# Forgetting attention in another order: long and short units in turn, negated scores with a running minimum, forget sums spread by one product of 40 rows

## The reference, cut to what matters

```python
q, k, v, z, f_logit = split(h @ w_in)                  # q, k, v: 8 heads x 128; f_logit: one per head
log_f = log_sigmoid(f_logit + b_f)
c = cumsum(log_f, axis=tokens)
s = einsum('bqhd,bkhd->bhqk', q_i, k) * 1/sqrt(128)    # for each block of 128 queries
logits = where(k_pos <= q_pos, s + c_q - c_k, -inf)
p = softmax(logits)
o = einsum('bhqk,bkhd->bqhd', p, v)
y = (o * silu(z)) @ w_out
```

## Time and profile before

| | |
|---|---|
| time, median of 3 runs | 2329.61 us (2328.22 to 2335.32) |
| the profiled execution's own time | 2328.99 us |
| its span in the trace | 2327.3 us, 29119 instructions |
| busy share of TensorE, VectorE, ScalarE, GpSimd | 95%, 48%, 37%, 18% |
| attention block: first score product to end of the last group's copy | 1586.37 to 1647.76 us |

### The profile page before, as it was taken

How to read it: one execution, slowest core, us unless ns; L and a number is a source line. 1 busy time by engine, 2 the same in 40 slices (tenths; PEclk the granted TensorE clock), 3 DMA queues, 4 the chain that set the end, 5 groups by cost and what they waited for, 6 DMA issues and landing times. The chain is left out here.

```text
span 2327.3 us, 29119 instructions
## 1 busy us (share of the span) xinstructions
PE 2208.1 (95%) x10778; PEld 1772.1 (76%) x10778; DVE 1124.9 (48%) x1810; ACT 855.8 (37%) x1407; POOL 417.6 (18%) x461
## 2 busy tenths in 40 slices
PE   7999999999889999998899989999999997999988
PEld 6888887766667888887788878886778887876657
DVE  5444324423436444324475544337656784655443
ACT  4322223443334322223432232135446743433453
POOL 2111002113333111001120010001100341014441
PEclk8999999999989999999899999999999997999999
DMA  4333333511022333331333246740243220242202
GB/s 136 115 92 98 93 100 84 95 46 55 19 73 73 108 91 99 91 99 52 103 98 90 82 76 108 98 80 1 73 119 82 55 55 20 76 97 60 52 19 67
DMA packets 359321, 182.10 MB, mean 78 GB/s; under 512 B 41926, under 2 KB 356015, under 8 KB 358831
## 3 DMA queue, kind: packets, MB, share of 16 engines
q1 hardware_dynamic: 359214, 180.69, 30.6%
HBM read 176.14 MB, written 4.52 MB: 78 GB/s over the span
## 5 line engine op out<-in xcount | busy, mean ns | idle before, releaser
L313 PE MATMUL ps<-xh,wh 128*128 128x512 f32 x1920 | 768.3, 400 | 12.9 <-DVE wl L280 10.9
L315 PE MATMUL ps<-xh,wl 128*128 128x512 f32 x1920 | 750.7, 391 | 0.0
L314 PE MATMUL ps<-xl,wh 128*128 128x512 f32 x1920 | 750.0, 391 | 0.0
L280 DVE TENSOR_TENSOR wl<-raw,wh 128x1024 fp32r<-128x1024 f32 x334 | 422.7, 1267 | 437.4 <-ACT wh L270 432.6
L270 ACT ACTIVATE wh<-raw 128x1024 fp32r<-128x1024 f32 x334 | 342.1, 1027 | 363.9 <-PE ps L315 332.6
L313 PEld LDWEIGHTS ps<-xh,wh 128*128 128x128 f32 x1920 | 361.9, 188 | 104.2 <-issue 18.2
L315 PEld LDWEIGHTS ps<-xh,wl 128*128 128x128 f32 x1920 | 361.6, 188 | 77.6
L314 PEld LDWEIGHTS ps<-xl,wh 128*128 128x128 f32 x1920 | 362.4, 189 | 73.6 <-issue 2.4
L457 PE MATMUL ps<-xh,wh 128*128 128x512 f32 x304 | 132.2, 435 | 26.2 <-ACT xh L392 15.5
L450 POOL TENSOR_TENSOR acc<-acc,sq 128x512 f32<-128x512 f32 x72 | 102.4, 1423 | 275.9 <-ACT sq L835 178.0
L314 PE MATMUL ps<-a_lo,wh 128*128 128x512 f32 x352 | 137.0, 389 | 0.0
(11 more groups left out here) (379 smaller groups left out, 2527.4 us busy)
## 6 DMA issues: line engine op xcount, KB each, us to landing
raw<-in_w_ffn_gate SPq DMA_DIRECT2D x44, 512.0 KB, 3.8
raw<-in_w_ffn_up SPq DMA_DIRECT2D x44, 512.0 KB, 3.8
raw<-in_w_ffn_down SPq DMA_DIRECT2D x32, 512.0 KB, 3.6
raw<-in_conv_w_in SPq DMA_DIRECT2D x32, 512.0 KB, 4.0
raw<-in_fox_w_in SPq DMA_DIRECT2D x32, 512.0 KB, 9.6
raw<-in_gdn_w_in SPq DMA_DIRECT2D x32, 512.0 KB, 4.1
raw<-in_w_in SPq DMA_DIRECT2D x24, 512.0 KB, 3.8
raw<-in_swa_w_in SPq DMA_DIRECT2D x32, 256.0 KB, 3.8
```

Source lines behind the costliest of these rows:

```text
L280: nc.vector.tensor_tensor(wl[s][:, 0:kb, :], raw[r][:, 0:kb, :], wh[s][:, 0:kb, :].bitcast(F32), ALU.subtract).then_inc(lo_done, 1)
L313: pe.matmul(o, wh[s][:, kb, :], x_hi, start=start, stop=False)
L314: pe.matmul(o, wh[s][:, kb, :], x_lo, start=False, stop=False)
L315: return pe.matmul(o, wl[s][:, kb, :], x_hi, start=False, stop=stop)
```

## The change

What it does, part by part:

- The order of the units: within each half of four heads, first k = 4 and k = 1 in turn (k = 4 of a head, k = 1 of the same head, then the next head), then k = 3 and k = 2 in turn. The group of a unit is given with the unit, and the groups end at other steps. Heads 4 to 7 are spread at steps 12, 14, 16 and 18 in place of 14, 15, 16 and 17.
- The sign: q is scaled by -128 ** -0.5, `nsel` holds +1 in place of -1, the mask fills +1e30. So Z is the negated score, the reduction takes the minimum, which is the negated maximum, and the exponential has scale -1. The instruction that negated the maximum (L1109) goes, and ScalarE waits for the reduction itself (`z_done`). `pair_steps` keeps its own instruction, and counts the semaphore from its own base (`n["maxima"]`, three lines not shown).
- The spread: the running sum is split by VectorE into a rounded high part and a rounded low part (three new instructions: copy, subtraction, copy, each of 8 x 512), on partitions 0 to 7 and 32 to 39 of `fhl`. `nsel` gets 40 rows with the selecting ones in both places, by two clears of zeros and two selects on GpSimd, and the product is one F32R instruction. The row of ones for the running sum is a broadcast of `ones`.

```diff
@@ -1052,16 +1052,12 @@
             U = len(units)
             Z, PT = room[:, 0:4, :], room[:, 4:6, :]
             SC, TR, PV = banks
-            cols = sb(f"{name}_cols", [P, 4, U], ctx=ctx)
-            MX, NM, RS, RI = range(4)
+            cols = sb(f"{name}_cols", [P, 3, U], ctx=ctx)
+            NM, RS, RI = range(3)
             B, BG = n["units"], n["groups"]
             n["units"] += U
             n["groups"] += len(groups)
-            group_of, start = {}, 0
-            for g, (last, _, _) in enumerate(groups):
-                for u in range(start, last + 1):
-                    group_of[u] = g
-                start = last + 1
+            group_of = {u: d["group"] for u, d in enumerate(units)}
             last_of = {last: g for g, (last, _, _) in enumerate(groups)}
             def pe_step(pe, s):
@@ -1104,10 +1100,7 @@
                     if u >= 4:
                         dve.wait_ge(t_done, B + u - 3)
                     nc.vector.tensor_tensor_reduce(Z[:, u % 4, 0:d["klen"]], ps[SC[u % len(SC)]][:, 0:d["klen"]], d["mask"],
-                                                   1.0, NEG, ALU.add, ALU.max, cols[:, MX, u:u + 1]).then_inc(z_done, 1)
-                    dve.wait_ge(z_done, B + u + 1)
-                    nc.vector.tensor_scalar(cols[:, NM, u:u + 1], cols[:, MX, u:u + 1], -1.0, None,
-                                            ALU.mult).then_inc(nm_done, 1)
+                                                   1.0, -NEG, ALU.add, ALU.min, cols[:, NM, u:u + 1]).then_inc(z_done, 1)
                 if 1 <= s < U + 1:
                     u, d = s - 1, units[s - 1]
                     dve.wait_ge(p_done, B + u + 1)
@@ -1120,9 +1113,9 @@
             def act_step(act, s):
                 if s < U:
                     u, d = s, units[s]
-                    act.wait_ge(nm_done, B + u + 1)
+                    act.wait_ge(z_done, B + u + 1)
                     z = Z[:, u % 4, 0:d["klen"]]
-                    nc.scalar.activation(z, z, ACT.Exp, bias=cols[:, NM, u:u + 1],
+                    nc.scalar.activation(z, z, ACT.Exp, bias=cols[:, NM, u:u + 1], scale=-1.0,
                                          accum_out=cols[:, RS, u:u + 1]).then_inc(p_done, 1)
                 if 2 <= s < U + 2:
                     u, d = s - 2, units[s - 2]
...
@@ -1811,9 +1805,11 @@
         with ExitStack() as c:
             qkv = sb("fox_qkvz", [P, 4 * DB, SEQ], ctx=c)
             vt = sb("fox_v", [P, TB, D], ctx=c)
-            fl = sb("fox_f", [H8, 4, SEQ], ctx=c)
+            fl = sb("fox_f", [H8, 3, SEQ], ctx=c)
             bf = sb("fox_bf", [H8, 1], ctx=c)
-            nsel = sb("fox_nsel", [H8, H8, P], ctx=c)
+            LO = 32
+            nsel = sb("fox_nsel", [LO + H8, H8, P], F32R, ctx=c)
+            fhl = sb("fox_f_parts", [LO + H8, SEQ], F32R, ctx=c)
             decay = sb("fox_decay", [P, 4, SEQ], ctx=c)
             f_in, fsel, fd, decay_mm, decay_in, bias_in = (sem(f"fox_{x}") for x in ("bf", "sel", "f", "rows", "decay", "bias"))
             ev0 = n["ev"]
@@ -1824,11 +1820,15 @@
             def pool_tail(pool):
-                nc.gpsimd.memset(nsel[:, :, :], 0.0).then_inc(fsel, 1)
-                nc.gpsimd.memset(fl[:, 3, :], 1.0).then_inc(fsel, 1)
-                pool.wait_ge(fsel, 1)
-                nc.gpsimd.affine_select(out=nsel[:, :, :], in_=nsel[:, :, :], compare_op=ALU.not_equal, fill=-1.0, base=0,
-                                        pattern=[[-1, H8], [0, P]], channel_multiplier=1).then_inc(fsel, 1)
+                nc.gpsimd.memset(nsel[:, :, :].bitcast(F32), 0.0).then_inc(fsel, 1)
+                nc.gpsimd.memset(fhl[:, :].bitcast(F32), 0.0).then_inc(fsel, 1)
+                pool.wait_ge(fsel, 2)
+                for part in range(2):
+                    if part:
+                        pool.wait_ge(fsel, 3)
+                    nc.gpsimd.affine_select(out=nsel[:, :, :], in_=nsel[:, :, :].bitcast(F32),
+                                            compare_op=ALU.not_equal, fill=1.0, base=-LO * part,
+                                            pattern=[[-1, H8], [0, P]], channel_multiplier=1).then_inc(fsel, 1)
             def f_evac(dve, i, j, ev0_):
                 if isinstance(i, int) and 4 * i + j == 28:
@@ -1842,7 +1842,7 @@
                 if 28 <= k < 32:
                     turn[0](pe, 2 * (k - 28), 2 * (k - 28) + 2)
                 if k >= 31:
-                    pe.wait_ge(fd, 6)
+                    pe.wait_ge(fd, 9)
                     for hd in (2 * (k - 31), 2 * (k - 31) + 1):
                         spread_decay(pe, hd)
@@ -1852,25 +1852,31 @@
                 if k in (28, 31):
                     q = qkv[:, 4 * (k > 28):4 * (k > 28) + 4, :]
                     dve.wait_ge(evac, ev0 + 8)
-                    nc.vector.tensor_scalar(q, q, P ** -0.5, None, ALU.mult)
+                    nc.vector.tensor_scalar(q, q, -(P ** -0.5), None, ALU.mult)
                 if k == 29:
                     dve.wait_ge(f_in, 16)
                     dve.wait_ge(evac, ev0 + 29)
                     nc.vector.tensor_scalar(fl[:, 0, :], fl[:, 0, :], bf[:, 0:1], None, ALU.add).then_inc(fd, 1)
                 if k == 30:
-                    dve.wait_ge(fsel, 3)
+                    dve.wait_ge(fsel, 4)
                     dve.wait_ge(fd, 4)
                     nc.vector.scalar_tensor_tensor(out=fl[:, 2, :], in0=fl[:, 0, :], scalar=0.0, in1=fl[:, 1, :],
                                                    op0=ALU.min, op1=ALU.subtract).then_inc(fd, 1)
                     dve.wait_ge(fd, 5)
-                    nc.vector.tensor_tensor_scan(fl[:, 0, :], fl[:, 3, :], fl[:, 2, :], 0.0, ALU.mult, ALU.add).then_inc(fd, 1)
+                    nc.vector.tensor_tensor_scan(fl[:, 0, :], ones[0:H8, 0:1].broadcast_to([H8, SEQ]), fl[:, 2, :], 0.0, ALU.mult, ALU.add).then_inc(fd, 1)
+                    dve.wait_ge(fd, 6)
+                    nc.vector.tensor_copy(fhl[0:H8, :], fl[:, 0, :]).then_inc(fd, 1)
+                    dve.wait_ge(fd, 7)
+                    nc.vector.tensor_tensor(fl[:, 1, :], fl[:, 0, :], fhl[0:H8, :].bitcast(F32), ALU.subtract).then_inc(fd, 1)
+                    dve.wait_ge(fd, 8)
+                    nc.vector.tensor_copy(fhl[LO:LO + H8, :], fl[:, 1, :]).then_inc(fd, 1)
             def spread_decay(pe, hd):
                 if hd >= 2:
                     pe.wait_ge(decay_in, hd - 1 if hd < 5 else hd)
-                pe.matmul(ps[7 if hd > 3 else 6 + hd % 2][:, :], nsel[:, hd, :], fl[:, 0, :], start=True, stop=True).then_inc(decay_mm, 1)
+                pe.matmul(ps[7 if hd > 3 else 6 + hd % 2][:, :], nsel[:, hd, :], fhl[:, :], start=True, stop=True).then_inc(decay_mm, 1)
             def copy_decay(act, hd):
                 act.wait_ge(decay_mm, hd + 1)
@@ -1901,18 +1907,19 @@
                     evac_dve=f_evac, loop_end=7)
             with ExitStack() as c2:
-                order = [(half, qb, hd) for half in range(2) for qb in range(TB) for hd in range(4 * half, 4 * half + 4)]
+                order = [(half, qb, 4 * half + x) for half in range(2) for two in ((3, 0), (2, 1)) for x in range(4) for qb in two]
+                done_order = [(half, qb) for half in range(2) for qb in (3, 0, 2, 1)]
                 bias_slot = [qkv[:, 22 + x, :] for x in range(2)]
                 units = []
                 for u, (half, qb, hd) in enumerate(order):
                     klen = (qb + 1) * P
                     units.append(dict(
                         q=qkv[:, hd, qb * P:qb * P + P], k=qkv[:, 8 + hd, 0:klen], klen=klen,
-                        mask=bias_slot[u % 2][:, 0:klen], mask_ready=(bias_in, u + 1), po=0, m=P,
+                        mask=bias_slot[u % 2][:, 0:klen], mask_ready=(bias_in, u + 1), po=0, m=P, group=done_order.index((half, qb)),
                         oc=(hd % 4) * P, v=[vt[:, x, hd * P:hd * P + P] for x in range(qb + 1)]))
-                second = {4 * TB + x - 2: 4 + x for x in range(4)}
+                second = {4 * TB + 2 * x - 4: 4 + x for x in range(4)}
                 def spread_second(pe, s):
                     if s in second:
@@ -1920,11 +1927,11 @@
                 def copy_second(act, s):
                     if s in second:
-                        act.wait_ge(bias_in, s + 2)
+                        act.wait_ge(bias_in, s - 2)
                         copy_decay(act, second[s])
-                groups = [(4 * g + 3, F[:, 4 * (g // TB):4 * (g // TB) + 4, (g % TB) * P:(g % TB) * P + P],
-                           lambda b: b[:, :].rearrange("p (a q) -> p a q", a=4)) for g in range(2 * TB)]
+                groups = [(order.index((half, qb, 4 * half + 3)), F[:, 4 * half:4 * half + 4, qb * P:qb * P + P],
+                           lambda b: b[:, :].rearrange("p (a q) -> p a q", a=4)) for half, qb in done_order]
                 u_fox = n["units"]
                 pe_p, dve_p, act_p = softmax_attention("fox", units, groups, qkv[:, 16:22, :], c2, spread_second, copy_second)
```

(9 more changed lines are left out.)

## The result

The changed kernel takes 2334.19 us in the median (2331.81 to 2342.11, 20 runs) against 2328.87 us for the kernel before beside it (2327.47 to 2335.32, 20 runs): the ratio is 1.0026, with a 95% interval of 1.002 to 1.0033. That is slower by 5.3 us, and within the 0.3% that were called no change; 2332.2 had been predicted.

A forecast was written before the change was run, and what follows sets the result against it. A two-unit cycle through ScalarE was taken to bound the block; start to 1594.7, 49.0 of cycles, 0.95 of spreads and 5.75 of end gave 1650.4 against 1647.76, +2.6 us: median 2332.2, range 2325 to 2338.

The forecast's parts named there:

- The cycle: In the block, reduction of s sets reduction of s + 2: 4.20 us per 4-1 pair, 3.38 per 3-2 pair.
- rival 3: Hand-over from reduction to ScalarE keeps its price of 0.31 us: +2.1 us, 2334 us; chance 0.15.
- The spreads: Four one-instruction F32R spreads ahead of long scores in the block: 0.24 us each, 0.95 in all.
- Ahead of the block: Split on VectorE, then two spreads in 0.48 us: tile 32 starts 0.35 us earlier, bounds 0 and 0.6.
- The start: Block's start: first reduction 1.6 us behind first scores, unit 4 reduced 7.1 us later, partly at half clock.
- The end: From unit 30's reduction to the block's end: 5.75 us, ending at 1650.4.
- middle: From unit 4 to unit 30 in the block: 13 cycles of 49.0 us plus 0.95 for spreads.
- The price of the order: Units in turn cost 1.2 and 0.4 us more a pair than sorted ones, over eight pairs each.
- 1 (throughput binds): In the block, engines' throughput binds, not the cycle: pairs of 2.8 us, 9 us less, 2321 us; chance 0.06.
- 2 (the clock falls in the middle): TensorE's clock falls inside the block: +13 us in all 4-1 stretches, 2345 us; chance 0.07.
- 4 (the minimum is slower): The block's minimum reduction takes a slower form, twice its 0.62 us on 13 cycles: +7 us, 2339; chance 0.02.
- 5: VectorE's scale reaches the shared memory port ahead of GpSimd's select, some 0.1 us earlier; no change in sum, no chance given.

The follow-up runs named there:

- e1: The kernel before with the new order of units alone, keeping maximum, negation and float32 spreads: 2336.94 us, ratio 1.0042 to the kernel before.
- e3: The changed kernel with ScalarE's copy of unit s - 2 put ahead of the exponential of unit s: 2323.42 us, ratio 0.9984 to the kernel before.
- e2: The changed kernel with the old sorted order of units and old spread steps, keeping minimum and F32R spread: 2321.64 us, ratio 0.9975 to the kernel before.
- e5: The changed kernel with ScalarE's copy ahead of the exponential and block spreads ahead of short scores: 2323.69 us, ratio 0.9987 to the kernel before.
- e6: The changed kernel with the old sorted order and steps, and ScalarE's copy ahead of the exponential: 2321.63 us, ratio 0.9976 to the kernel before.
- e12: The changed kernel measured once more, unaltered: 2334.16 us, ratio 1.0027 to the kernel before on the same chip.
- e7: The kernel before with negated scores and the minimum alone, no negation instruction, old order and spreads: 2322.40 us, ratio 0.9978 to the kernel before.
- e8: The kernel before with the F32R spreads alone, keeping sorted order, maximum and negation: 2325.31 us, ratio 0.999 to the kernel before.
- e10: The changed kernel with ten unread F32R products in TensorE's idle time ahead of the block: 2334.06 us, ratio 1.0025 to the kernel before.
- e11: e6 with unread TensorE products, ten ahead of the block and others behind it: 2319.67 us, ratio 0.9962 to the kernel before.

## Why the prediction was right, and where it was off

**The cycle: right.** Long units set the pace with nothing idle between: 4.14 and 3.36 us a pair, 4.20 and 3.38 predicted. Its parts: the hand-over from the reduction is 0.12 (0.15 taken, so rival 3 with 0.31 is out), that from the copy to the values 0.05 (0.15 taken), copy, exponential and scores as priced. The values took 1.00 (0.92 taken), which ate most of what the hand-overs gave: the sum is better than its terms. e1 and e3 show it from both sides: with the negation in it a 4-1 pair takes 4.33 us, and with the copy taken out of it 3.28.

**The spreads: the mis-sized term.** "0.24 each", with up to 0.5 kept for gaps; on the cycle one takes 3.98 - 3.36 = 0.62 us, against a pair of the same sizes without one. 0.43 lie between the spread and the scores behind it, 0.1 ahead of it (values to spread 0.87, values to scores 0.77), 0.1 behind (scores to reduction 0.95 for 0.85). 24 like products in a row show 0.24 each, and don't show the price of standing alone between others. Four spreads: +1.5 us. A float32 one costs 1.25 on the same cycle (e1), so the gain is a half, not three quarters.

**Ahead of the block: right, with luck.** From running sum to first score it takes 12.38 us for 12.75, -0.37 (-0.35 predicted). Two misses cancel: the spreads start 2.88 behind the start of the running sum (3.03 taken), and both take 0.66 (0.48 taken).

**The start: off by 0.4.** The first reduction comes 1.13 behind the first score (1.6 taken), unit 4 7.93 behind unit 0 (7.1 taken). The clock fell later than before, 5 us behind the first score in place of 0.6, and the half clock covered the scores of unit 4 as well as the values of unit 0:

```profile
1589.12 2.08 PE L1087 MATMUL ps<-fox_qkvz,fox_v 128*128 128x128 f32 x8 [0.60 <-ACT fox_qkvz L1125]
1590.99 1.77 PE L1069 MATMUL ps<-fox_qkvz 128*128 128x512 f32 x2
```

They take 1.16 and 1.02 at full clock; the prediction had 1.1 for the scores. The end was right, 5.84 for 5.75.

**The sum.** Start -0.47, unit 4 +0.83, middle 50.94 for 49.96 (+0.98: the spreads' 1.5 less half a microsecond of hand-overs), end +0.09: the block is 1.4 us longer than predicted, so +4.1 for +2.6 with the scatter of the running sum taken out. That the whole came out at 2333.7 for 2331.6 is luck in part: of the profiled execution's +4.7 us, +4.1 is this, +2.6 lies behind the block and 0.3 outside the span, where the prediction had nothing, and the early running sum takes 2.3 off.

**The price of the order.** The prediction says that turns cost 1.2 and 0.4 us more a pair, over eight pairs each, 12.8 in all. The runs show 8.3 (e1) and 9.9 (after against e2): units in sorted order don't run at the formula's pace either. Nothing in the forecast was worked out from this figure.

**The rivals.** 1 (throughput binds) was false for the queues as they are, and comes close once the copy goes first, for 3-2 pairs: 2.88 us for its 2.8 to 2.9, while 4-1 pairs still take 3.28. 2 (the clock falls in the middle) was false: 1.00 from 1593 to 1645. The rule cited for it, from the Trainium skill's page "TensorE: Matmul & The Clock Gate", section "A second HAM failure mode: psum-queue depth-cycling", isn't borne out there, with a gap of 0.60 and one of 0.31 in each 4-1 pair. 4 (the minimum is slower) was false: the reduction of 512 takes 0.69, as before. 5 happened: the scale starts 0.19 behind the reduction's end and the select 0.29. With sorted units (e2) the scale of 512 then takes 0.49 us where it took 0.80, and the select of 512, now the later one, 0.81 in the mean where it took 0.61. The Trainium skill, page "SBUF — State Buffer", section "SBUF: two separate sides", has the pair of ports as a lock for whoever comes first. These numbers agree: the one that comes second grows longer. Off the cycle, as with units in turn, no gain from it shows.

**What stays open.** By its block the change costs 4.1 us; the medians differ by 5.3 and 6.7. Behind the block the changed kernel takes 682.1 us in both traces, before 679.5, and e3, e5 and e6 took 681.2 to 682.5, which is also where their block's gains of 6.7, 7.8 and 8.2 shrank to 3.8, 4.2 and 6.3 in the medians. The clock right behind the block doesn't explain it (e12), and 0.3 lies outside the span. Most of the rest lies in one place, 508 us behind the block, in the projection of the sliding window attention. The last line of each fence is a window, as in the earlier trace rows. The kernel before:

```profile
2155.60 0.66 PE L1201 MATMUL ps<-ident,swa_z 128*128 128x128 f32 x4 [1.42 <-POOL swa_z L1253]
...
2156.60:2159.60 3.00, 3.00 (x22) 1.80 (x18) 0.40 (x3) 0.75 (x3) 0.36 (x2) 1.00 0.00 0
```

The changed kernel at the same place:

```profile
2156.09 0.17 DVE L1234 RECIPROCAL swa_cols<-swa_cols 128x2 f32<-128x2 f32 x1 [0.29 <-issue]
...
2158.24 0.66 PE L1195 MATMUL ps<-ident,swa_z 128*128 128x128 f32 x4 [1.78 <-POOL swa_z L1247]
...
2159.20:2162.20 3.00, 3.00 (x12) 1.95 (x8) 0.00 (x0) 0.78 (x3) 0.40 (x2) 0.50 0.00 0
```

One small VectorE instruction starts 0.29 us late with nothing to wait for, GpSimd and with it TensorE's transposes come later, TensorE is idle for 1.78 us in place of 1.42, and behind this the granted clock is 0.50 in place of 1.00. From the split of the weight tile ahead of it to that of the next one ScalarE takes 15.16 us there, for 13.28 before: 1.9 us. All ten traces of kernels that have both the minimum and the F32R spreads show the gap and the fall, with 1.77 or 1.78 us and a clock of 0.50; the four that don't have both (before, e1, e7, e8) have 1.42 or 1.43 us and 1.00. The medians point the same way, though they scatter by as much: e7 and e8 gain 5.5 and 2.6 us, e2, which has both, only 5.6. Why that instruction starts late in these kernels, and whether the longer gap is what lets the clock fall, was not tested.

## What to carry to other kernels

When everyone waits for somebody, look for a cycle in the timeline and count how many units it spans; with a cycle over two units, putting long and short in turn makes all long ones share one, and the short ones' slack is lost. Before reordering the work, try the order inside one engine's step: here one exchanged pair of ScalarE instructions was worth 10.8 us of the block, more than the order cost. And compare what follows a changed part as well: here nearly 2 us went 500 us behind it. Price a lone product with its changes of operands, from a place where it stands alone, not from the middle of a row of its like.

## What the hardware did that was not expected

- A lone F32R product of 40 rows and 512 columns costs 0.62 us on the cycle between float32 products; in a row of 24 F32R products of 128 rows and 512 columns each takes 0.24.
- VectorE's scale of 512 elements takes 0.49 us when it starts 0.10 ahead of GpSimd's select (e2), and took 0.80 when it started 0.09 behind it. Dropping the negation, 0.15 us long, turned that round.
- The clock fell some 5 us into the block with or without 2.56 us of products ahead of it (e10), but not in e11. From the first score on TensorE was busy for 3.95 of 6 us in e10 and for 4.41 in e11, and then for 8.19 and 10.00 of the next ten, where e10's stretch holds the fall itself.
- The same clock fell 508 us behind the block in ten traces of fourteen, each time behind 1.77 or 1.78 us of idle TensorE, and not in the four where this was 1.42 or 1.43.
- Every kernel with the F32R spreads spends 2.0 us or more outside its span, every other one 1.7.
